# A three-block sequence model on one core: a layer norm's loads and adds moved into the stage before it, turns of two projections pipelined, and the input stages reordered

## The reference, cut to what matters

```python
def first_block(x, ...):                       # stick-breaking attention, 16 heads of 64
    h = x + attention(rms_norm(x, norm_mix))
    h = h + swiglu(rms_norm(h, norm_ffn), ffn_w_in, ffn_w_out)
    h = h + sigmoid(rms_norm(h, norm_ple) @ ple_w_gate) * (p @ ple_w_proj)
    return rms_norm(h, final_norm)

def second_block(x, c, ...):
    u = rms_norm(x, norm_g) * (1 + scale) + shift      # from silu(c) @ ada_w
    a = conv_a * sigmoid(conv_b)                       # all slices of u @ w_in
    a = causal_depthwise_conv(a)                       # width 31
    a = silu(_layernorm(a, conv_ln_g, conv_ln_b))      # mean and variance over 1024 channels
    y_conv = (a @ conv_pw) * silu(conv_gate)
    y_ret = groupnorm(retention(rotary(q), rotary(k), v)) * silu(ret_gate)   # 4 heads
    h = x + gate * (concat(y_conv, y_ret) @ w_out)
    return rms_norm(h, final_g)

def third_block(x, p, ...):
    u_s5, z_s5, z_ssd, xBC, dt = split(rms_norm(x, norm_w) @ w_in)
    y_s5 = gelu(s5_scan(u_s5))                         # 64 groups of 16 channels, complex states
    y_s5 = y_s5 * sigmoid(y_s5 @ w_glu + b_glu) * silu(z_s5)
    y_ssd = gated_norm(ssd(silu(causal_conv4(xBC)), dt), z_ssd)
    h = x + concat(y_s5, y_ssd) @ w_out
    h = h + (p @ w_ple_proj) * sigmoid(rms_norm(h, ple_norm_w) @ w_ple_gate)
    return rms_norm(h, final_norm_w)
```

## Time and profile before

| | |
|---|---|
| times of three runs | 4280.0, 4285.0, 4288.73 us, median 4285.0 |
| profiled execution | 4283.41 us; its span in the trace 4281.6 us |
| TensorE's granted clock over the span | 0.932 |
| TensorE busy | 3896.8 us, 91% of the span, 19274 matmuls |
| weight loads (beside matmuls) | 3153.5 us, 74% |
| VectorE busy | 2194.4 us, 51% |
| GpSimd busy | 1040.4 us, 24% |
| ScalarE busy | 900.6 us, 21% |

### The profile page before, as it was taken

One profiled execution on the slowest core, in us unless ns is written; L12 is line 12 of the kernel. 1 busy time (PEld: TensorE's weight loads), 2 busy tenths in 40 slices (PEclk: granted clock), 3 DMA queues, 4 the chain that ended last, 5 costly groups with the idle time before them and its releaser, 6 DMA issues.

```text
span 4281.6 us, 47901 instructions
## 1 busy us (share of the span) xinstructions
PE 3896.8 (91%) x19274; PEld 3153.5 (74%) x19274; DVE 2194.4 (51%) x2811; ACT 900.6 (21%) x1636; POOL 1040.4 (24%) x581
## 2 busy tenths in 40 slices
PE   7899999899999998999899997698989698889898
PEld 6677676688888887888777685576778577777777
DVE  3455546433333266999324432445235984753555
ACT  2434334200000032111011001302111112542032
POOL 1111211334344432333211220022222231003222
PEclk9999999999999999999999998799999897879999
DMA  2000000211112111222210212011562134212111
GB/s 76 25 26 21 30 25 16 64 64 57 65 54 68 58 46 35 86 86 83 72 42 30 69 50 74 20 59 42 142 105 83 55 103 133 59 60 79 59 45 64
DMA packets 139192, 260.23 MB, mean 61 GB/s; under 512 B 45584, under 2 KB 87568, under 8 KB 135952
## 3 DMA queue, kind: packets, MB, share of 16 engines
q1 hardware_dynamic: 72208, 156.26, 12.7%
q10 hardware_dynamic: 66816, 101.63, 7.0%
HBM read 209.35 MB, written 46.14 MB: 60 GB/s over the span
## 4 chain that ended last, share of the span: by engine, by line
PE 81%; DVE 11%; ACT 3%; issue 2%; DMA 1%; POOL 1%; ACTq 1%; SPq 0%; DVEq 0%; POOLq 0%
PE bank L555 22%; PE bank L557 21%; PE bank L556 21%; PE bank L674 2%; PE bank L804 2%; PE bank L937 2%; PE bank L767 2%; PE bank L926 1%; PE bank L1066 1%; PE bank L787 1%; DVE hn L1782 1%; DVE xl L1793 1%; DVE fb L1925 1%; DVE s5t L2263 1%; DVE h L2264 1%
## 5 line engine op out<-in xcount | busy, mean ns | idle before, releaser
L555 PE MATMUL bank<-xh,wh 128*128 128x512 f32 x3008 | 1201.0, 399 | 121.0 <-ACT xc L1576 39.5
L556 PE MATMUL bank<-xl,wh 128*128 128x512 f32 x3008 | 1185.0, 394 | 0.0
L557 PE MATMUL bank<-xh,wl 128*128 128x512 f32 x3008 | 1183.5, 393 | 0.0
L512 POOL CAST wh<-raw 128x1024 fp32r<-128x1024 f32 x264 | 281.8, 1067 | 3136.2 <-PE bank L557 3081.6
L555 PEld LDWEIGHTS bank<-xh,wh 128*128 128x128 f32 x3008 | 573.8, 191 | 282.5 <-issue 85.6
L514 POOL TENSOR_TENSOR wl<-raw,wh 128x1024 fp32r<-128x1024 f32 x264 | 672.7, 2548 | 21.1
L557 PEld LDWEIGHTS bank<-xh,wl 128*128 128x128 f32 x3008 | 572.9, 190 | 122.3
L556 PEld LDWEIGHTS bank<-xl,wh 128*128 128x128 f32 x3008 | 574.1, 191 | 115.0
L2068 DVE SCALAR_TENSOR_TENSOR bank<-apad,cols,bank 128x512 f32<-128x512 f32 x406 | 267.9, 748 | 0.0
L1829 DVE TENSOR_TENSOR h<-bank,h 128x512 f32<-128x512 f32 x240 | 165.7, 691 | 159.4 <-PE bank L557 158.5
L1925 DVE TENSOR_TENSOR_SCAN fb<-fb 128x256 f32<-128x256 f32 (+7 forms) x128 | 186.5, 1498 | 106.7 <-ACT ab L1254 106.7
(11 more groups left out here) (340 smaller groups left out, 5520.4 us busy)
## 6 DMA issues: line engine op xcount, KB each, us to landing
raw<-in_wstream SPq DMA_DIRECT2D x264, 512.0 KB, 3.6
spills<-spill ACTq DMA_DIRECT2D x40, 512.0 KB, 2.7
rawm<-in_mod_w ACTq DMA_DIRECT2D x12, 1024.0 KB, 5.0
gate_spill<-gates ACTq DMA_DIRECT2D x16, 512.0 KB, 2.6
tabs<-in_rope ACTq DMA_DIRECT2D x4, 2048.0 KB, 8.4
f<-spills SPq DMA_DIRECT2D x8, 1024.0 KB, 5.9
h<-in_x ACTq DMA_DIRECT2D x4, 1024.0 KB, 12.0
tabs<-gate_spill ACTq DMA_DIRECT2D x4, 1024.0 KB, 7.3
```

Source lines behind the costliest of these rows:

```text
L512: nc.gpsimd.tensor_copy(wh[:, slot], raw[:, slot]).then_inc(S("panel_high"), 1)
L555: nc.tensor.matmul(o, lh, rh, start=start, stop=False)
L556: nc.tensor.matmul(o, lh, rl, start=False, stop=False)
L557: return nc.tensor.matmul(o, ll, rh, start=False, stop=stop)
```

## The change

1. *Start.* ADDED_TILES gets "mix": 8: VectorE adds the input's squares. The small Silu work on `c` moves ahead of the squares. The S5 coefficients (VectorE) move behind the first four entries of ATTN_START, the exponentials (ScalarE) behind the first two.
2. *Attention.* The scores' second half for g + 2 goes ahead of `values(g)`.
3. *Layer norm.* `cv` is loaded in four pairs of tiles, three pairs issued by ScalarE in the last retention head, once the buffers whose memory they take (`qr`, `kr`, `vt`) are done with, and the fourth, in the place of `ot`, once `rl` is made. VectorE adds a tile to the mean behind every two units of that head's output. Centring goes tile by tile, ScalarE squares each as it comes, VectorE adds the squares of six.
4. *Turns.* pw and glu run in0 in1 out0 in2 out1 in3 out2 out3; `yh`, `yl`, `vh`, `vl` hold four tiles instead of two, and the weights' order in HBM follows.
5. *Third block.* Six xbc tiles come ahead of the z tiles, S5 kernel p starts in z tile p, `product(n)` stands behind xbc tile n + 7, and the second four `next_run` behind tiles 6 and 7.

```diff
+XBC_FIRST = 6
...
-    ("conv", KT, 4, 8), ("ret", 1, 8 * RET_HEADS, 28 * RET_HEADS), ("pw", 4, 4, 20),
-    ("s5_u", 4, 2, 4), ("s5_z", 4, 2, 4), ("ssd_z", 4, 2, 4), ("xbc", 8, 2, 4), ("dt", 1, 2, 2),
-    ("ssd_out", 4, 2, 4), ("glu", 4, 4, 20),
+    ("conv", KT, 4, 8), ("ret", 1, 8 * RET_HEADS, 28 * RET_HEADS), ("pw", 1, 16, 80),
+    ("s5_u", 4, 2, 4), ("xbc_first", XBC_FIRST // 2, 2, 4), ("s5_z", 4, 2, 4), ("ssd_z", 4, 2, 4),
+    ("xbc", 8 - XBC_FIRST // 2, 2, 4), ("dt", 1, 2, 2),
+    ("ssd_out", 4, 2, 4), ("glu", 1, 16, 80),
...
+TURN_ORDER = [("in", 0)] + [x for i in range(4) for x in ([("in", i + 1)] if i < 3 else []) + [("out", i)]]
...
+CONV_LOADS = [2, 4, 0, 6]
...
-S5_FIRST = 2
-S5_OUT_AFTER = {5: 0, 7: 1, 9: 2, 10: 3, 11: 4, 12: 5, 13: 6, 14: 7}
+S5_OUT_AFTER = {n + 7: n for n in range(8)}
...
-ADDED_TILES = {"ffn": 6, "ple": 6, "first_final": 6, "second_final": 4, "ple3": 6, "last_final": 6}
+ADDED_TILES = {"mix": 8, "conv_ln": 6, "ffn": 6, "ple": 6, "first_final": 6, "second_final": 4, "ple3": 6, "last_final": 6}
...
+                scores(g + 2, 1)
                 values(g)
-                scores(g + 2, 1)
...
+                for kind, i in TURN_ORDER:
+                    unit, panel = turn_unit(name, kind, i), panels(name) + TURN_PANEL[kind, i]
+                    if kind == "in":
+                        for m in range(2):
+                            tile_x(unit + 2 * m, panel + m, in_high, in_low,
+                                   split=split if i == 0 and m == 0 else None)
+                    else:
+                        pe.wait_ge(S(sem), i * 4 + 4)
+                        s = slice(2 * (i % 2), 2 * (i % 2) + 2)
+                        out_two(unit, panel, high[:, s], low[:, s], norm if i == 3 else None)
...
+                for e in range(XBC_FIRST):
+                    tile_x(xbc_unit(e), xbc_panel(e))
...
                     tile_x(units(name) + 2 * m, panels(name) + m,
-                           between=(lambda: s5_kernel(n)) if 0 <= n < KT else None)
-                    if 0 <= n - 1 < KT:
-                        s5_inputs(n - 1)
-                for e in range(16):
+                           between=(lambda: s5_kernel(p)) if p < KT else None)
+                    if 0 <= p - 1 < KT:
+                        s5_inputs(p - 1)
+                for e in range(XBC_FIRST, 16):
...
-            act.wait_ge(S("eps"), 1)
-            for k in range(KT):
-                act.wait_ge(S(f"x_in{k // 2}"), 16)
-                norm_square("mix", k)
-            norm_root("mix")
-            norm_highs("mix")
...
-            act.wait_ge(S("s5_small_in"), 16)
-            A(s5c[:, 3, :], s5c[:, 2, :], ACT.Exp).then_inc(S("s5_act"), 1)
...
+            act.wait_ge(S("eps"), 1)
+            for k in range(KT):
...
+            for key in ATTN_START[:2]:
+                attn_take(key)
+            act.wait_ge(S("s5_small_in"), 16)
+            A(s5c[:, 3, :], s5c[:, 2, :], ACT.Exp).then_inc(S("s5_act"), 1)
+            act.wait_ge(S("s5_angles"), 1)
+            A(s5c[:, 5, :], s5c[:, 4, :], ACT.Exp).then_inc(S("s5_act"), 1)
...
+            for key in ATTN_START[2:]:
                 attn_take(key)
...
+                if n == RET_HEADS - 1:
+                    act.wait_ge(S("conv_stored1"), KT // 2 * 16)
+                    for k in CONV_LOADS[:3]:
+                        act.dma_start(cv[:, k:k + 2, :], conv_spill[k:k + 2].rearrange("k p t -> p k t")
+                                      ).then_inc(S(f"pair_in{k // 2}"), 16)
...
+                else:
+                    act.wait_ge(S("rl_ready"), n * 2 + 2)
+                    k = CONV_LOADS[3]
+                    act.dma_start(cv[:, k:k + 2, :], conv_spill[k:k + 2].rearrange("k p t -> p k t")
+                                  ).then_inc(S(f"pair_in{k // 2}"), 16)
...
             if "pw" in run:
                 all_evicted(act, "ret")
-                act.wait_ge(S("conv_stored1"), KT // 2 * 16)
-                act.dma_start(cv[:, :, :], conv_spill.rearrange("k p t -> p k t")).then_inc(S("cv_in"), 16)
-                act.wait_ge(S("ln_centered"), 2 * KT)
                 for k in range(KT):
+                    act.wait_ge(S("ln_centered"), 2 * k + 2)
                     norm_square("conv_ln", k, cv)
...
+                for i in range(4):
+                    unit = turn_unit("pw", "in", i)
+                    if i:
+                        for u in (2, 3):
+                            evicted(act, turn_unit("pw", "in", i - 1) + u)
...
+                    if i >= 2:
+                        produced(act, turn_unit("pw", "out", i - 2) + 15)
...
-                            A(yh[:, m, th * HALF:(th + 1) * HALF], yt[:, th, :], ACT.Copy
+                            A(yh[:, 2 * (i % 2) + m, th * HALF:(th + 1) * HALF], yt[:, th, :], ACT.Copy
...
-                        if th == 0 and 0 <= n < KT:
-                            s5_kernel(n)
...
+                for e in range(XBC_FIRST):
+                    take_xbc(e)
+                silu(XBC_FIRST - 1)
+                for p in range(16):
...
+                        if th == 0 and p < KT:
+                            s5_kernel(p)
...
+                    if 0 <= p - 1 < KT:
+                        s5_inputs(p - 1)
+                for e in range(XBC_FIRST, 16):
+                    take_xbc(e)
...
+                    if then is not None:
+                        then(n)
...
+            dve.wait_ge(S("c_ready"), 3)
+            V.tensor_tensor(cl[:, :, :], cf[:, :, :], ch[:, :, :].bitcast(F32), ALU.subtract
+                            ).then_inc(S("cl_ready"), 1)
+            for k in range(KT):
+                norm_add("mix", k)
             norm_inverse("mix")
             norm_split("mix", gain("norm_mix"))
...
-            dve.wait_ge(S("s5_small_in"), 16)
-            s5_coefficients()
...
-            for key in ATTN_START:
+            for key in ATTN_START[:4]:
+                attn_take(key)
+            dve.wait_ge(S("s5_small_in"), 16)
+            s5_coefficients()
...
+            def conv_total(n):
+
+                tiles = [k + m for k in CONV_LOADS for m in range(2)]
+                if n + 1 == KT:
+                    return
+                dve.wait_ge(S(f"pair_in{tiles[n + 1] // 2}"), 32)
+                if n == 0:
+                    V.tensor_tensor(acc[:, :], cv[:, tiles[0], :], cv[:, tiles[1], :], ALU.add
+                                    ).then_inc(S("mean_acc"), 2)
+                    return
+                dve.wait_ge(S("mean_acc"), n + 1)
+                V.tensor_tensor(acc[:, :], acc[:, :], cv[:, tiles[n + 1], :], ALU.add).then_inc(S("mean_acc"), 1)
...
-                add_tiles(ret_unit("out", n), lambda n: mod[:, 16 + n:17 + n])
+                add_tiles(ret_unit("out", n), lambda n: mod[:, 16 + n:17 + n], then=conv_total if n == RET_HEADS - 1 else None)
...
-                dve.wait_ge(S("cv_in"), 16)
-                V.tensor_tensor(acc[:, :], cv[:, 0, :], cv[:, 1, :], ALU.add).then_inc(S("mean_acc"), 2)
...
-                    V.tensor_tensor(acc[:, :], acc[:, :], cv[:, k, :], ALU.add
...
-                for th in range(2):
-                    dve.wait_ge(S("mean_sum"), th + 1)
-                    for k in range(KT):
+                for k in range(KT):
+                    for th in range(2):
...
+                    if k:
+                        norm_add("conv_ln", k - 1)
...
+                for kind, i in TURN_ORDER:
+                    unit = turn_unit("pw", kind, i)
+                    if kind == "out":
+                        add_tiles(unit, lambda n: mod[:, 16 + n:17 + n], norm="second_final" if i == 3 else None)
+                        continue
...
+                            if i or m:
+                                dve.wait_ge(S("yl_ready"), i * 4 + 2 * m + th - 1)
...
-                    add_tiles(unit + 4, lambda n: mod[:, 16 + n:17 + n], norm="second_final" if last else None)
...
+                dve.wait_ge(S("zeroed"), 3)
+                for e in range(XBC_FIRST):
+                    xbc_taps(e)
...
-                for e in range(16):
...
-                    if e in (1, 3):
-                        next_run(e + 3)
-                        next_run(e + 4)
+                for e in range(XBC_FIRST, 16):
+                    xbc_taps(e)
+                    if e < XBC_FIRST + 2:
+                        for g in range(2):
+                            next_run(4 + 2 * (e - XBC_FIRST) + g)
...
+                for kind, i in TURN_ORDER:
+                    unit = turn_unit("glu", kind, i)
+                    if kind == "out":
+                        add_tiles(unit, half_way=(lambda: side_low(2)) if i == 3 else None,
+                                  norm="ple3" if i == 3 else None)
+                        continue
...
+    for kind, c in TURN_ORDER:
+        stream += [pw[2 * c], pw[2 * c + 1]] if kind == "in" else list(o2[c])
...
-    stream += list(tiles(w3[:, :5 * D]))
```

(2 more changed lines are left out.)

160 lines of the change are left out of this document (70 added, 90 removed).

## The result

The changed kernel takes 4152.1 us (median of four runs, 4146.42 to 4155.8), the kernel before 4282.5 in the same comparison. The ratio is 0.9699, with a 95% interval of 0.9678 to 0.972. The forecast was 4147. The profiled execution has a span of 4151.6 us, 130.0 less than before's.

The account below looks back on a forecast made before the run. The prediction took TensorE, 81% of the chain, to bound the kernel, with only its waits and slow clock reducible. Terms 24 + 12 + 34 + 20 + 18 + 28 = 136 us, from 4283.4 to 4147, range 4122 to 4184.

Parts of the forecast that it names:

- Start: Kernel start: input scaling begins at about 30.2 us instead of 42.99, query-tile hole goes; 24 us less, bounds 10 to 27.
- Attention: Attention: moved scores fill seven TensorE waits for at, 10.5 us, plus some clock; 12 us less, bounds 0 and 20.
- Layer norm: Layer norm after the last head's output: 67.2 us becomes 29.8; after a 3 us charge 34 us less, bounds 20 and 38.
- Turns: pw and glu turns: shorter TensorE waits; 20 us less in pw (bounds 10, 27), 18 in glu (bounds 8, 30).
- Third block: Third block: DMA wait goes, xc hole mostly filled, new wait for pb; 28 us less, bounds 12 and 34.
- The 3 us charged for adds that meet GpSimd: Last head's output: 3 us taken off the layer norm's gain for one add stretched beside GpSimd's panel split.
- rival A: Turns, attention, norm: stalls shrink but TensorE's clock stays slow; 24 us less gained, 4171 us; chance 0.17.
- The DMA wait: Third block, first S5 kernel: TensorE's 10.34 us wait goes, with 4 us of slow clock behind it, 14.5 us.
- the prediction's scale: Third block: times counted from the end of s5_u (3073) as zero.
- one meeting with GpSimd: Third block, VectorE's way from the scans to product(0): 2 us allowed for meeting GpSimd once.
- xc hole: Third block: TensorE's 37.1 us wait for ScalarE's xc is filled but for 3 us.
- The wait for pb: Third block, before s5_outputs(0): a new TensorE wait of 20 to 25 us, with product(0) ready at 370.6.

Follow-up runs that it names:

- e2: The changed kernel with the input's squares summed by TensorE again instead of added by VectorE: 4166.94 us, ratio to before 0.973.
- e3: The changed kernel with the S5 coefficients and exponentials ahead of the first query and key tiles again: 4165.1 us, ratio to before 0.9734.
- e1: The changed kernel with the second half of attention's scores for g + 2 behind values(g) again: 4172.39 us, ratio to before 0.9751.
- e11: The changed kernel with the seven adds for the layer norm's mean behind the last head's output, not inside it: 4165.71 us, ratio to before 0.9737.
- e6: The changed kernel with two xbc tiles ahead of the z tiles instead of six: 4155.59 us, ratio to before 0.9699.
- e10: The changed kernel with GpSimd making only an eighth of the weight panels' low parts for z and later xbc tiles (wrong products): 4129.15 us, ratio to before 0.9647.

## Why the prediction came out right, step by step

**Start (24, measured 25.0).** The scaling was to start at 30.2 and starts at 29.98. e2 and e3 show both halves to be real, 11.8 and 8.5 us when each is undone alone; with the 1.5 us of the table load they leave some 3 us of the 25.0 that no run assigns.

**Attention (12, measured 20.8).** The mechanism was right and the size was not. The moved scores were credited with 10.5 us for the waits of 1.45 to 2.2 us, seven of them, and 1.5 us for the clock. e1 shows 15.5 us of idle time and 3.2 of clock. The smaller waits for `at` shrank too: 15 places with 21.9 us became 8 with 8.1. Counting only the seven large ones was the fault. The stretch is 0.8 us over the bound of 20; of its 20.8 us, e1 gives 18.7 to the order, and the other 2.1 are within the spread of this stretch.

**Layer norm (34, measured 37.2).** The forecast had 29.8 us from the output's end to the scaling; it is 28.9. The 3 us charged for adds that meet GpSimd were too many: the output took 1.15 us longer. e11 shows that it pays to have them there.

**Turns (20 and 18, measured 12.0 and 13.2).** The new waits were forecast as 2.5 and 3.9 us and are 2.44 and 3.79. What failed is the step from wait to gain. The prediction let a pw place lose 7.2 us before (10.0 less 2.8) and gain 4.2 of them, so that the new wait of 2.5 and 0.5 us of slow clock would remain, and in glu it did the same. The slow stretch did not shrink like that. It begins behind the new wait with a granted clock of 0.76 over 7 us, which is an estimated 1.7 us lost, against 1.5 to 2.7 us at the four places before. So a shortened place in pw gives little more than the difference of the waits, some 2.2 us. This is rival A at these six places. It did not hold for attention, where most of the waits vanished altogether.

**Third block (28, measured 18.4).** The DMA wait went, as forecast (e6 brings it back). The first DMAs start at 87.8 us on the prediction's scale instead of 82, the last product is at 231.0 instead of 228. Then the scans, taken over from before at 106.2 us to the next taps, take 114.9. That is the step that failed (e10): it priced one meeting with GpSimd behind the scans and none of the three new ones inside them. So the xc hole is 13.2 us and not 3. The wait for pb was to be 20 to 25 and is 19.1. It ends at 380.6 instead of 370.6. The 18.4 us come from single traces of both kernels; with the shortest of the seven traces of the same code it would be 23.9, still under 28.

The terms missed by +1, +9, +3, -8, -5 and -10 us, which is -10 in sum. The stretches forecast as unchanged gave 3.4 in this one trace. The total owes its 5 us to errors of both signs.
